# Feed-forward blocks of a two-layer stack: the products over tokens by Strassen, seven of 256 tokens in place of eight

## The reference

```python
def swiglu(h, w_gate, w_up, w_down):
    return (jax.nn.silu(h @ w_gate) * (h @ w_up)) @ w_down
...
x = x + swiglu_ffn(rms_norm(x, norm_ffn_g), w_ffn_in, w_ffn_out)             # fa
...
x = x + 0.5 * swiglu(rms_norm_2(x, ffn1_norm), ffn1_gate, ffn1_up, ffn1_down) # fb
...
x = x + 0.5 * swiglu(rms_norm_2(x, ffn2_norm), ffn2_gate, ffn2_up, ffn2_down) # fc
```

## Time and profile before

| | us |
|---|---|
| median of 3 runs | 2423.3 |
| lowest, highest | 2423.14, 2424.0 |
| profiled execution: first to last instruction (span) | 2420.5 |
| what lies around the span, run's median less span | 2.8 |
| TensorE (PE) busy | 2397.5 |
| VectorE (DVE) busy | 1263.9 |
| ScalarE (ACT) busy | 1002.5 |
| GpSimd (POOL) busy | 331.9 |

### The profile page before, as it was taken

How to read it: one execution, slowest core, us unless ns; L and a number is a source line. 1 busy time by engine, 2 the same in 40 slices (tenths; PEclk the granted TensorE clock), 3 DMA queues, 4 the chain that set the end, 5 groups by cost and what they waited for, 6 DMA issues and landing times.

```text
span 2420.5 us, 30412 instructions
## 1 busy us (share of the span) xinstructions
PE 2397.5 (99%) x12064; PEld 1956.4 (81%) x12064; DVE 1263.9 (52%) x1907; ACT 1002.5 (41%) x1634; POOL 331.9 (14%) x258
## 2 busy tenths in 40 slices
PE   8999999999999999999999999999999999999998
PEld 7777778777898888888888888888887888888887
DVE  5688746468765455443333544333678555333422
ACT  7766654234563344333223433222644454323321
POOL 0000000555100100111102111101032201101100
PEclk9999999999999999999999999999999999999999
DMA  6221235323665232332323332332322232333231
GB/s 203 71 70 51 86 99 183 113 68 108 200 210 209 96 105 70 105 95 88 96 97 101 99 97 90 96 100 88 111 63 63 87 113 74 101 96 105 97 100 56
DMA packets 172638, 251.65 MB, mean 104 GB/s; under 512 B 11472, under 2 KB 90576, under 8 KB 172496
## 3 DMA queue, kind: packets, MB, share of 16 engines
q1 hardware_dynamic: 171344, 248.13, 32.5%
q10 hardware_dynamic: 1152, 1.57, 0.2%
HBM read 231.83 MB, written 16.78 MB: 103 GB/s over the span
## 4 chain that ended last, share of the span: by engine, by line
PE 96%; DVE 2%; ACT 1%; issue 0%; POOL 0%; DMA 0%; DVEq 0%; SPq 0%; POOLq 0%
PE bank L1170 94%; PE bank L1299 1%; DVE wlo L2030 0%; PE bank L1322 0%; DVE T L2038 0%; PE bank L1447 0%; PE bank L1423 0%; DVE macc L2030 0%; PE bank L1265 0%; DMA raw<-in_w_in 0%; DVE xg L2034 0%; ACT whi L1541 0%; DVE ml L2038 0%; DVE bank L2336 0%; DVE W L2030 0%
## 5 line engine op out<-in xcount | busy, mean ns | idle before, releaser
L1170 PE MATMUL bank<-xh,whi 128*128 128x512 f32 x1784 | 710.1, 398 | 8.0 <-DVE wlo L2030 8.0
L1170 PE MATMUL bank<-xh,wlo 128*128 128x512 f32 x1784 | 696.6, 390 | 0.0
L1170 PE MATMUL bank<-xl,whi 128*128 128x512 f32 x1784 | 695.9, 390 | 0.0
L2030 DVE TENSOR_TENSOR wlo<-raw,whi 128x1024 fp32r<-128x1024 f32 (+2 forms) x406 | 500.2, 1234 | 337.2 <-ACT whi L1541 337.0
L1541 ACT ACTIVATE whi<-raw 128x1024 fp32r<-128x1024 f32 (+2 forms) x406 | 419.2, 1038 | 513.7 <-PE bank L1170 507.2
L1170 PEld LDWEIGHTS bank<-xh,whi 128*128 128x128 f32 x1784 | 335.7, 188 | 94.7 <-issue 20.2
L1170 PEld LDWEIGHTS bank<-xh,wlo 128*128 128x128 f32 x1784 | 335.4, 188 | 71.1
L1170 PEld LDWEIGHTS bank<-xl,whi 128*128 128x128 f32 x1784 | 336.0, 188 | 65.4
L2030 DVE TENSOR_TENSOR T<-bank,R 128x512 f32<-128x512 f32 x86 | 59.0, 687 | 344.3 <-PE bank L1170 344.3
L1170 PE MATMUL bank<-hh,whi 128*128 128x512 f32 (+1 forms) x536 | 206.9, 386 | 0.0
L1170 PE MATMUL bank<-hl,whi 128*128 128x512 f32 (+1 forms) x536 | 206.8, 386 | 0.0
(11 more groups left out here) (356 smaller groups left out, 3494.9 us busy)
## 6 DMA issues: line engine op xcount, KB each, us to landing
raw<-in_w_in SPq DMA_DIRECT2D x92, 512.0 KB, 3.6
raw<-in_w_ffn_in SPq DMA_DIRECT2D x88, 256.0 KB, 3.2
raw<-in_ffn_gate SPq DMA_DIRECT2D x88, 256.0 KB, 2.8
raw<-in_ffn_up SPq DMA_DIRECT2D x88, 256.0 KB, 3.1
raw<-in_ffn_down SPq DMA_DIRECT2D x44, 512.0 KB, 3.6
raw<-in_w_ffn_out SPq DMA_DIRECT2D x22, 512.0 KB, 3.6
raw<-in_w_xattn_kv SPq DMA_DIRECT2D x16, 512.0 KB, 4.4
raw<-in_w_kv_mem SPq DMA_DIRECT2D x16, 512.0 KB, 4.9
```

The source lines that it names most:

```text
L1170: return e.matmul(out, l, r, start=start, stop=stop, skip_group_check=skip)
L2030: return e.tensor_tensor(out, a, b, op)
```

## The change

The three feed-forward blocks are built anew; all else stays but for addresses. A **unit** is 256 output columns against 8 slices of 128 rows on the way out (G for gate, U for up), or against 8 (phase 0 and 1) or 6 (phase 2) slices of h on the way back (D, four per phase). In a unit the weights are 2 x 2 blocks of 128 x 128 per pair of slices, and the operand is 2 x 2 blocks (two slices, two halves of 256 tokens). Winograd's form of Strassen's algorithm has seven products of such blocks for eight:

- POOL makes four sums of weight blocks per unit (w_add). The blocks and sums are then split by ACT (s_hi) and DVE (s_lo) in the groups k1, k2, 12 and 4: 1024, 1024, 1024 and 512 elements per partition for four pairs of slices, where it was two slots of 1024.
- The operand has four sums as well (op_sum) and is split in two parts (op_hi, op_lo): for x once per block, for h with each U unit.
- TensorE does seven products of 4 x 3 matmuls of 256 tokens (product), in three banks. Products 6, 7 and 4 add to what 1 has left in its bank, 3 to what 5 has left. ACT copies the states between to memory (take), and DVE adds up the four output blocks (c11, c22, c21, c12). In a G unit POOL multiplies by R in four steps where it was two of 512; in a U unit DVE multiplies by the gates (h_mul, c21). In a D unit DVE adds every product to x at once (x_add), with the later ones of a bank holding the earlier ones.
- The order of a steady unit u, with v behind it, is products 6, 5, 7, 2, 4 of u, 1 of v, 3 of u. The sums of a unit's weights are ordered two units ahead.
- Plain (no sums) are the first G and U unit of a block and all four D units of phase 2. There the second slices of the pairs have matmuls of 512 tokens, the first slices two of 256, since the halves of the operand lie apart (whole).
- h is no longer kept: four tiles hold the slices of one phase, and the way back is done in three phases between the pairs of the way out: pairs 0 to 3 and G4, D, U4 to pair 7 and G8, D, U8 to pair 10, D.
- A raw unit of 1 MB has one of three buffers and is loaded in two transfers. Memory below the old base is used too.

```diff
-BASE = 17408
+SCRATCH = 1024
+BASE = SCRATCH + 1024
...
-        hh = [at_kb(118 + 2 * j, [P, S], F32R, name="hh") for j in range(22)]
-        hl = [at_kb(162 + 2 * j, [P, S], F32R, name="hl") for j in range(22)]
+        wraw = [at_kb(kb, [P, 4, 2, 256], name="wraw") for kb in (0, 8, 202)]
...
+        wh1 = [at_kb(kb, [P, 4, 256], F32R, name="wh1") for kb in (16, 216)]
+        wh2 = [at_kb(kb, [P, 4, 256], F32R, name="wh2") for kb in (40, 24)]
+        wh12 = [at_kb(kb, [P, 2, 4, P], F32R, name="wh12") for kb in (20, 28)]
+        wh4 = [at_kb(kb, [P, 4, P], F32R, name="wh4") for kb in (38, 44)]
...
+        hop = [at_kb(146 + 14 * i, [P, 14, 256], name="hop") for i in range(4)]
...
+        def units(tag, out, g, gc, u, uc, down, loc):
+            order = []
+            for ph, (first, last) in enumerate(((0, 4), (4, 8), (8, 11))):
+                for p in range(first, last):
+                    order += [("G", p, ph)] if p in (0,) or p not in (4, 8) else []
+                    order += [("U", p, ph)]
+                order += [("G", last, ph + 1)] if last < 11 else []
+                order += [("D", i, ph) for i in range(4)]
...
+        def operands(key, k, plain=False):
+            h = int(key[0] == "h")
+            if not plain and (h or key == "fc" or key == "fa"):
+                step("op_sum", key, k)
+            soon(h, "op_hi", key, k, 0)
+            soon(2 * h, "op_lo", key, k, 0)
+            if plain or not h:
+                soon(h, "op_hi", key, k, 2)
+                soon(1 + h, "op_lo", key, k, 2)
+            if not plain:
+                if key == "fb":
+                    soon(3, "op_sum", key, k)
+                soon(3 if h else 4, "op_hi", key, k, 1)
+                soon(4 if h else 5, "op_lo", key, k, 1)
...
+            if p in (1, 6, 7):
+                if p == 1:
+                    q = PAIR[u]
+                    for j in range(2):
+                        tmp.new("ffn", u, j, among=((0, 2, 4)[q] + j,))
+                step("take", u, p)
+                if p == 7:
+                    step("c22", u)
+                    if kind == "G":
+                        step("gate_r", u, "c22")
+            elif p == 2:
+                step("c11", u)
+                if kind == "G":
+                    step("gate_r", u, "c11")
+            elif p == 4:
+                step("c21", u)
+                if kind == "G":
+                    soon(1, "gate_silu", u, 1)
+                    soon(2, "gate_r2", u, 1)
+                else:
+                    step("h_mul", u, 0)
+            elif p == 3:
+                step("c12", u)
+                if kind == "G":
+                    step("gate_r", u, "c12")
+                    soon(1, "gate_silu", u, 0)
+                    soon(1, "gate_r2", u, 0)
+                else:
+                    step("h_mul", u, 1)
+                    operands(("h", u), i, i > 7)
...
+                plan = [[], [(v2, add(1)), (v, hi("k2"))], [(v, lo("12")), (v2, add(3)), (v2, add(2)), (v3, LOAD[0])],
+                        [(v, hi("4")), (v, lo("k2")), (v2, add(4))], [(v, lo("4"))], [(v2, hi("k1")), (v3, LOAD[1])],
+                        [(v2, lo("k1")), (v2, hi("12"))], []]
+                if plain:
+                    plan[1] = [(v, hi("k1"))] + plan[1]
+                    plan[2] = [(v, lo("k1")), (v, hi("12"))] + plan[2]
+                order = [(1, u), (5, u), (6, u), (2, u), (7, u)] if plain else [(6, u), (5, u), (7, u), (2, u), (4, u)]
+                order += [] if UN[v]["plain"] else [(1, v)]
+                order += [(4, u), (3, u)] if plain else [(3, u)]
+                for k, (p, y) in enumerate(order):
+                    product(y, p)
+                    for z, what in plan[k] + (sum(plan[k + 1:], []) if (p, y) == (3, u) else []):
+                        want(z, what)
+                n, plain = n + 1, False
...
+            def product(u, p, kts):
+                x = UN[u]
+                kind, g = x["kind"], WEIGHT_OF[p]
+                first, last = kts[0] == 0, kts[-1] == x["nk"] - 1
+                ring, name = (main, "alpha") if p in (1, 4, 6, 7) else (side, "gamma") if p == 2 else (main, "beta")
+                n, b = ring(name, u)
+                fresh = p in (1, 2, 5)
+                if first and fresh:
+                    w.wait_ge(*(free(main, "main", n) if ring is main else free(side, "side", n)))
+                if first and p == 6:
+                    w.wait_ge(*at("taken", u, 1))
+                if first and p == 7:
+                    w.wait_ge(*at("taken", u, 6))
+                if first and p == 4:
+                    w.wait_ge(*at("taken", u, 7))
+                if first and p == 3:
+                    w.wait_ge(*at("taken", u, 5))
+                w.wait_ge(*at("s lo", u, g))
+                a, c = hi_tile(u, g), raw_view(u, g, True)
+                if g == "12":
+                    a, c = (t[:, 0 if p == 5 else 1] for t in (a, c))
+                elif g in ("k1", "k2"):
+                    cols = slice(0, P) if p in (1, 2) else slice(P, 256)
+                    a, c = a[:, :, cols], c[:, :, cols]
+                out, slot = b[:, 0:256], SLOT_OF[p]
+                for kt in kts:
+                    key, k = operand_at(u, kt)
+                    w.wait_ge(*at("op lo", key, k, int(slot < 4)))
+                    r = operand_tiles(key, k)[1]
+                    begin, end = fresh and kt == 0, kt == x["nk"] - 1
+                    mm(out, a[:, kt, :], r[:, 7 + slot, :], begin, False, skip=not fresh)
+                    mm(out, a[:, kt, :], r[:, slot, :], False, False, skip=not fresh)
+                    ins = mm(out, c[:, kt, :], r[:, 7 + slot, :], False, end, skip=not fresh)
+                if last:
+                    ins.then_inc(*up("gemm", ("product", u, p)))
...
+            def whole(u, m, kts, half):
...
+                    for i, group in ((1, "k2"), (0, "k1")):
+                        w.wait_ge(*at("s lo", u, group))
+                        a, c = hi_tile(u, group)[:, kt, chunk(m)], raw_view(u, group, True)[:, kt, chunk(m)]
+                        begin = half in (None, 1) and i == 1 and kt == (2 if half else 0)
+                        end = i == 0 and kt == x["nk"] - 1
+                        parts = [(b[:, 0:256], r[:, 11, :], r[:, 4, :]), (b[:, 256:512], beside_[:, 0, :], beside_[:, 1, :])]
+                        if i:
+                            wide = [r[:, j:j + 2, :].rearrange("p a b -> p (a b)") for j in (12, 5)]
+                            parts = [(b[:, 0:512], *wide)]
...
+                        for out, h, l in parts:
+                            mm(out, a, h, begin, False, skip=True)
+                            mm(out, a, l, False, False, skip=True)
+                            ins = mm(out, c, h, False, end, skip=True)
...
+                src = raw_view(u, g)
+                copy(hi_tile(u, g), src).then_inc(*up("w_hi", ("s hi", u, g)))
+            def take(u, p):
+                x = UN[u]
+                n, b = main("alpha", u)
+                for j in range(2):
+                    w.wait_ge(*free(tmp, "tmp", tmp("ffn", u, j)[0]))
+                t = half_views(u)
+                out = {1: t[0][:, 0:256], 6: t[0][:, 256:512], 7: t[1][:, 256:512]}[p]
+                w.wait_ge(*at("product", u, p))
+                copy(out, b[:, 0:256]).then_inc(*up("taken", ("taken", u, p)))
...
+            def s_lo(u, g):
...
+                tt(raw_view(u, g, True), raw_view(u, g), hi_tile(u, g).bitcast(F32), ALU.subtract).then_inc(
+                    *up("w_lo", ("s lo", u, g)))
+            def c11(u):
+                n, b = side("gamma", u)
+                t = half_views(u)[0][:, 0:256]
+                w.wait_ge(*at("taken", u, 1))
+                w.wait_ge(*at("product", u, 2))
+                tt(t, b[:, 0:256], t, ALU.add).then_inc(*up("blocks", ("c11", u), ("side", "free", n)))
...
+            def h_mul(u, part):
+                g, t = gate_of(u), hop[UN[u]["i"] % 4]
+                (up0, up1), (gate0, gate1) = half_views(u), half_views(g)
+                if part == 0:
+                    w.wait_ge(*at("c22", u))
+                    tt(t[:, 10, :], up1[:, 256:512], gate1[:, 256:512], ALU.mult)
+                    w.wait_ge(*at("gate r2", g, 0))
+                    w.wait_ge(*at("c11", u))
+                    tt(t[:, 8, :], up0[:, 0:256], gate0[:, 0:256], ALU.mult)
+                    return
+                w.wait_ge(*at("c12", u))
+                tt(t[:, 7, :], up0[:, 256:512], gate0[:, 256:512], ALU.mult).then_inc(
+                    *up("blocks", ("h mul", u), *[("tmp", "free", tmp("ffn", y, j)[0]) for y in (u, g) for j in range(2)]))
...
+                if i == 1:
+                    w.wait_ge(*at("unit there", u))
+                    if x["loc"] < 5:
+                        w.wait_ge(*at("w used", x["base"] + 3))
+                    for event in done(ago(u, 2), 5, 6):
+                        w.wait_ge(*event)
```

(17 more changed lines are left out.)

## The result

| us | before | after |
|---|---|---|
| median of 4 runs | 2423.4 | 2584.5 |
| lowest, highest | 2423.1, 2424.0 | 2582.8, 2584.9 |
| ratio, 95% interval | | 1.0665 (1.065 to 1.0681) |
| span of the profiled execution | 2420.5 | 2582.5 |
| mean granted clock of TensorE | 0.998 | 0.979 |

A forecast was written before the change was run, and what follows sets the result against it. TensorE, busy 2397.5 of 2420.5 us, was taken as the bound. 2420.5 - 62.8 (matmuls) + 72 (collision) + 15 (copies) = 2444.7 us of span, 2447.5 us with the 2.8 between span and median; forecast range 2428 to 2505.

The forecast's parts named there:

- TensorE's term: Feed-forward blocks: fewer multiplications by Strassen's algorithm save 62.8 us on TensorE if nobody makes it wait.
- The collision: Feed-forward blocks: DVE operations with both inputs in SBUF and POOL operations hold each other up, costing 72 us.
- the turns: Steady pair, way out: times DVE and POOL hold each other up sum to 24.8 us against TensorE's 20.16.
- rival B: Pairs of the way out: mutual waits in in-order queues lose 2.5 us more per pair, 2522 us; chance 0.13.
- The last three pairs of a block: Way out, h plain: DVE and POOL sum to 22.5 us per pair, 2.3 too many.
- head start: Each of three entries into a stretch of pairs brings 5 us, taking 39 us per block to 24.
- The clock, hidden: Pairs of the way out: a granted clock of 0.91 gives 22.2 us, still under 24.8, so costs nothing by itself.
- Entry, joints and end: Block entry, joints between blocks and the end: 0, at most 3 us either way.
- ACT's copies: Products into the same bank wait for ACT's copy out of PSUM: 5 us per block, 15 in all.
- The door that was forecast: Late POOL sums reach TensorE through DVE's combinations, which free the banks and stand behind waiting low parts.
- Rival A: Feed-forward blocks: TensorE stays the bound, pairs under 22.25 us, kernel faster at 2361 to 2418 us; chance 0.37.
- the signs that were named: Way out: 24 to 26 us per pair, PE below 85%, DVE and POOL both above 90%.

The follow-up runs named there:

- e12: Changed kernel with each POOL weight sum replaced by one constant memset, measured four times in turn with the kernel before: 2404.9 us, ratio 0.9926.
- e2: Changed kernel with each POOL weight sum replaced by three constant memsets, longer than a sum but reading nothing: 2417.2 us.
- e10: Changed kernel with each POOL weight sum replaced by a POOL copy of one block, which reads SBUF: 2426.9 us.
- e1: Changed kernel with each POOL weight sum replaced by one constant memset of the same tile, single run: 2407.1 us.
- e6: Changed kernel with the gate units' weight sums moved to DVE and POOL's multiplications by R in Strassen gate units left out: 2478.5 us.
- e4: Changed kernel with POOL's five multiplications by R per Strassen gate unit left out: 2513.5 us.
- e3: Changed kernel, full computation, with all four weight sums per unit moved from POOL to DVE: 2539.3 us.
- e5: Changed kernel, full computation, with the gate units' weight sums moved to DVE and the others left on POOL: 2557.0 us.

## Why the prediction was wrong in size

**TensorE's term, -62.8: right.** Matmuls of 256 tokens start 120 ns apart; two rows of the timeline of after with 24 starts between them, 2.88 us:

```profile
1110.34 0.29 PE L1446 MATMUL bank<-hopr,wrawl 128*128 128x256 f32 x1
...
1113.22 0.28 PE L1446 MATMUL bank<-hopr,wlastl 128*128 128x256 f32 x1
```

and a pair without the weight sums takes 20.2 us (e12).

**The collision, +72: right in kind, too small.** After is 180 us over the same kernel with memsets for the sums (e12). That the turns are the mechanism is shown by e2 and e10 against after. The stretches of pairs of the three blocks have 176 us more than 20.16 per pair (22.4 for a plain one), the norms taken off, where 72 were forecast; e12 has 11 there. The 104 us between 72 and 176 have three parts:
- *The steady pair, some +37.* Its turns were worked out as 24.8 us, 4.6 over TensorE; it takes 26.5, 6.3 over, in seven pairs of each block. The 1.7 more point to turns that are lost as well, as rival B had it with 2.5. By the two timelines neither such an operation of DVE nor one of POOL is under way for 0.9 us of the pair; the other 0.8 may as well be turns priced too low. One place where turns are lost: in the pair from 1166.7 POOL's multiplication by R waits for DVE, ACT's silu for the multiplication, ACT's copy stands behind the silu and a high part, and DVE waits for the copy (start, us, what, idle before):

```profile
1173.42 0.63 ACT L2300 ACTIVATE pair<-pair 128x512 f32<-128x512 f32 x1 [1.67 <-POOL pair L3312]
...
1175.37 0.42 DVE L2435 TENSOR_TENSOR pair<-bank,pair 128x256 f32<-128x256 f32 x1 [2.63 <-ACT pair L1864]
```

The experiments say the same. Ordered by turns per pair (e1 16.8, e6 20.2, e4 21.5, e3 22.2, e5 23.5, after 24.8) the times stand in order too, 2407, 2478, 2513, 2539, 2557 and 2584. But over e1, and for each of 30 pairs, they are 2.4, 3.5, 4.4, 5.0 and 5.9 us, where the turns exceed 20.16 by 0.0, 1.3, 2.0, 3.3 and 4.6: always 1.3 to 2.4 more, the borders' share included.
- *The last three pairs of a block, some -10.* Their stretch has 3.5 of surplus where 2.3 for each was worked out.
- *The borders of the stretches, some +77: the step that failed most.* *"I let each of the three entries into a stretch of pairs ... bring 5 us of head start"* took 45 us off; what came was 32 on top.

The borders one by one:
- Behind the way back the head start came: 21.2 us for the first pair, 5.3 less than for the next.
- Behind the plain pair it didn't. POOL's timeline there (start, us, what, idle before):

```profile
989.97 2.16 POOL L3312 TENSOR_TENSOR wlast<-wraw,wsum 128x512 f32<-128x512 f32 x1
997.44 1.38 POOL L3312 TENSOR_TENSOR pair<-pair,R 128x512 f32<-128x512 f32 x1 [5.32 <-ACT pair L2300]
999.65 1.82 POOL L3312 TENSOR_TENSOR pair<-pair,R 128x512 f32<-128x512 f32 x1 [0.83 <-ACT pair L2300]
1002.83 1.30 POOL L3312 TENSOR_TENSOR wsum<-wraw 128x512 f32<-128x512 f32 x1 [1.36 <-DMA wraw<-in_w_ffn_in]
```

One unit's sums are done ahead; then POOL idles, and the next unit's sums begin at 1002.83, when their load has landed and their pair has started. Eight sums then stand in a row until 1016.5, beside DVE's sums and low parts of h. The pair takes 30.0 us: no head start, and 3.5 on top. I had looked at POOL's room there and not at whether its data were in.
- At the end of a stretch the last pair takes 3.5 more than a steady one: PE waits 3.44 for DVE's first sum into x of the way back. No term had this.
- x's own sums and low parts, which I had counted nowhere, lie beside the plain pair. In fa it takes 24.95 us where 22.4 were worked out, but PE is never idle there: the norm's short matmuls take 1.3, and the granted clock is 0.94 behind the wait at the entry, so little is left for x's. In fb it takes 28.5. How the 9 us more of fb's first stretch come about is open.

**The clock, hidden: not settled.** *"A clock like that by itself is hidden, since 20.16/0.91 = 22.2 is still under 24.8"*. In the steady pair PE's busy time grew by 2.2 us at a granted clock of 0.94, and e12 has 1.00 and no growth. But these 2.2 and the 4.1 of idle are PE's account of the same 6.3 us; they don't say what a full clock would have saved. The wait of 2.63 above stood behind ACT's queue, not behind a slow product. On the other side POOL waits 1.84 us in that pair for a product before it may start a sum, and there a late PE can come back. No run holds the clock fixed, so its share of the 6.3 is open. Over the span busy is 65.6 us more than worked out. By the mean clocks, 0.979 and 0.998, and two levels of 2.4 and 1.2 GHz, some 108 us were spent at the lower one instead of 10, half of which, 49, is lost; the rest of the 65.6 I can't assign, since ends of matmuls are modelled. Most of the clock's part disappears with the waits (e12: busy 2348.9, granted 0.992).

**Entry, joints and end, 0: wrong.** With no weight sum left (e12) 44 us remain over TensorE's term, for which 0, at most 3, was put. PE waits 6.07 us at the entry to fa for the low part of the first unit, and 6.55 ahead of the last plain unit of fa's way back:

```profile
1377.32 1.19 PE L1446 MATMUL bank<-hopr,wh 128*128 128x512 f32 x2 [6.55 <-DVE wrawl L2435]
```

e1 has three of these, 19.4 us, without any weight sum: they come from the order of the steps. With the slower clock behind them they make up most of the 44. At the entry to fa the unit's low part stands in DVE's queue behind a low part of x, which waited 2.31 us for ACT, and takes 2.28 itself beside POOL's sums of x:

```profile
974.30 1.40 DVE L2435 TENSOR_TENSOR xopr<-xop,xopr 128x768 fp32r<-128x768 f32 x1 [2.31 <-ACT xopr L1864]
975.62 2.28 DVE L2435 TENSOR_TENSOR wrawl<-wraw,wh 128x1024 fp32r<-128x1024 f32 x1
```

**ACT's copies, +15: about 0 of their own.** PE's 64.2 us of waiting for them goes with the sums (e1). *"If PE mostly waits for ACT's copies, the small term was the large one"* was the wrong sign to look for: the copy is the door by which the late sum reaches PE. The door that was forecast, DVE's combinations behind its low parts, was there too, for 35.1 us (1.4 in e12). The 25.2 us behind low parts themselves are mostly no late sums: e1 still has 19.4 of them.

**Rival A** fails on its own condition: 26.5 us per pair where it decides at 22.25. Of the signs that were named, 24 to 26 us per pair came as 26.5, PE below 85% as 84.5, DVE above 90% as 90; POOL, put above 90%, has 76%, which fits lost turns too.

In sum: 72 + 15 were forecast against the 62.8; what came is 225 (159 idle, 66 busy): 180 with the weight sums and 44 without them. The forecast is 137 under, 108 by the collision and 44 by entries and joints, less the 15 for copies. The three blocks, 409.3, 411.6 and 400.7 us against 338.2, hold 202 of the 225 (the norms' 5 taken off), and the waits at their entries (6.07 and 6.56 us at fa and fc), which lie ahead of them, are among the other 23.

## What to carry to other kernels

Add up the turns of every pair of engines that share an access before the engines one by one: here four engines each had room under TensorE, and the sum of two of them didn't. Take that sum as a floor: the steady pair took 1.7 us more than it, and e6, whose turns just fit, still lost 71 us. A surplus in a steady stretch is to be taken for every repetition; credit for slack at its borders needs a look at what has landed by then. Where TensorE waited it also worked slower behind the wait (49 us here by the granted clock). To price a helper's operation, replace it by one that writes as much and reads nothing: that one run told length from contention.

## What the runs showed of the hardware

- A short operation pays the most. DVE's product of gate and up of 256 elements takes 0.42 in e3 and 0.89 in after, beside POOL's sums; its sum of 256 in h, `hop<-hop`, 0.425 in e1 and 1.298 in after. A low part of 1024 went from 1.26 (e1) to 1.64.
- POOL's memset of 512 elements takes 526 ns in the mean of each group of e1 and e2 (1008 in e2), with DVE's two-input operations beside it; a copy of the same size takes 0.61 at its shortest in e10 and 0.96 to 1.25 in the mean of its groups.
- DVE's combinations of 256 elements with one input in PSUM have 411 to 421 ns in the mean in every version.
